# Seven block products instead of eight in the first feed-forward matrix, with fewer filler matmuls at the start

## The reference, cut to what matters

```
h2 = rms_norm(x, norm2[l]) * (1.0 + sc2) + sh2
hidden = jnp.square(jax.nn.relu(h2 @ w_ff1[l]))      # (512 x 1024) @ (1024 x 4096)
x = x + gt2 * (hidden @ w_ff2[l])                    # (512 x 4096) @ (4096 x 1024)
```

## Time and profile before

| | |
|---|---|
| median of 3 runs | 3221.87 us |
| the profiled execution | 3222.51 us |
| its span in the trace | 3220.8 us |
| TensorE matmul busy | 3208.4 us (100%), 15398 matmuls |
| VectorE busy | 1898.4 us (59%) |
| ScalarE busy | 1157.6 us (36%) |
| GpSimd busy | 239.1 us (7%) |
| granted TensorE clock | 0.999 |

### The profile page before, as it was taken

The page is one execution under the profiler, slowest core; times in us unless marked ns, Lnnn a source line. Parts: engine busy times, 40 slices in busy tenths (PEclk is TensorE's granted clock), DMA queues, the critical chain, the costliest instruction groups (busy, mean ns, idle before and its releaser), DMA issues.

```text
span 3220.8 us, 43689 instructions
## 1 busy us (share of the span) xinstructions
PE 3208.4 (100%) x15398; PEld 2653.5 (82%) x15398; DVE 1898.4 (59%) x2738; ACT 1157.6 (36%) x1534; POOL 239.1 (7%) x250
## 2 busy tenths in 40 slices
PE   9999999999999999999999999999999999999998
PEld 8788888888888788888888888768888888888887
DVE  8455557554447455567564445666665744586656
ACT  4433343332223433333332223354333523553423
POOL 2100000100001100000100002051000101320001
PEclk9999999999999999999999999999999999999999
DMA  7246325322222146325422222202222322122222
GB/s 266 67 167 209 120 96 171 136 98 96 93 98 99 63 163 206 129 92 169 141 95 98 98 98 90 79 27 102 101 98 96 107 98 92 47 79 99 97 98 79
DMA packets 100012, 358.89 MB, mean 111 GB/s; under 512 B 11056, under 2 KB 13360, under 8 KB 99760
## 3 DMA queue, kind: packets, MB, share of 16 engines
q1 hardware_dynamic: 98960, 354.08, 31.5%
q0 software_dynamic: 928, 3.17, 0.3%
HBM read 355.11 MB, written 2.10 MB: 111 GB/s over the span
## 4 chain that ended last, share of the span: by engine, by line
PE 99%; DVE 1%; ACT 0%; DVEq 0%; issue 0%; ACTq 0%; POOL 0%; POOLq 0%
PE pb L625 25%; PE pb L626 25%; PE pb L627 25%; PE pb L657 2%; PE pb L658 2%; PE pb L661 2%; PE pb L695 2%; PE pb L696 2%; PE pb L697 2%; PE pb L1014 1%; PE pb L1388 1%; PE pb L1389 1%; PE pb L1390 1%; PE pb L920 1%; PE pb L1004 1%; PE pb L921 1%
## 5 line engine op out<-in xcount | busy, mean ns | idle before, releaser
L1460 ACT ACTIVATE hi<-raw 128x1024 fp32r<-128x1024 f32 x548 | 576.4, 1056 | 983.4 <-PE pb L627 674.1
L2010 DVE TENSOR_TENSOR lo<-raw,hi 128x1024 fp32r<-128x1024 f32 x548 | 668.5, 1224 | 352.6 <-ACT hi L1460 307.8
L625 PE MATMUL pb<-yH,hi 128*128 128x512 f32 (+1 forms) x1664 | 645.1, 388 | 0.0
L626 PE MATMUL pb<-yL,hi 128*128 128x512 f32 (+1 forms) x1664 | 644.8, 388 | 0.0
L627 PE MATMUL pb<-yH,lo 128*128 128x512 f32 (+1 forms) x1664 | 644.8, 388 | 0.0
L625 PE MATMUL pb<-hH,hi 128*128 128x512 f32 x1512 | 590.7, 391 | 0.0
L626 PE MATMUL pb<-hL,hi 128*128 128x512 f32 x1512 | 589.2, 390 | 0.0
L627 PE MATMUL pb<-hH,lo 128*128 128x512 f32 x1512 | 589.1, 390 | 0.0
L626 PEld LDWEIGHTS pb<-yL,hi 128*128 128x128 f32 x1664 | 312.6, 188 | 63.5
L627 PEld LDWEIGHTS pb<-yH,lo 128*128 128x128 f32 x1664 | 312.6, 188 | 63.5
L625 PEld LDWEIGHTS pb<-yH,hi 128*128 128x128 f32 x1664 | 312.7, 188 | 63.3
(11 more groups left out here) (438 smaller groups left out, 4038.8 us busy)
## 6 DMA issues: line engine op xcount, KB each, us to landing
raw<-stream SPq DMA_DIRECT2D x648, 512.0 KB, 3.3
yF<-first SPq DMA_DIRECT2D x8, 512.0 KB, 12.3
act<-first SPq DMA_DIRECT2D x8, 512.0 KB, 15.6
x<-xT SPq DMA_DIRECT2D x4, 512.0 KB, 6.4
outT<-act SPq DMA_DIRECT2D x7, 256.0 KB, 2.2
act<-crow POOLq DMA_DIRECT2D x2, 512.0 KB, 5.6
tab<-decay SPq DMA_DIRECT2D x1, 1024.0 KB, 8.1
scr<-ws POOLq DMA_DIRECT2D x2, 256.0 KB, 3.1
```

The source lines that it names most:

```text
L625: pe.matmul(out, whi, ahi, start=first, stop=False)
L626: pe.matmul(out, whi, alo, start=False, stop=False)
L1460: act.activation(hi[:, s], raw[:, s], ACT.Copy).then_inc(hi_ready, 1)
L2010: dve.tensor_tensor(lo[:, s, 0:width], raw[:, s, 0:width], hi[:, s, 0:width].bitcast(F32), ALU.subtract).then_inc(lo_ready, 1)
```

## The change

**Block products.** In slabs two to four, two weight tiles are worked together as a group. The weights of a group are cut in four quarters (`raw[:, s0]` and `raw[:, s1]` hold the two output blocks, each with its two inner halves), and the input h2 (`hH`, `hL`) is cut in inner half by token half. Seven products of quarters take the place of eight. Each product is 4 inner blocks x 3 matmuls, of 128 x 256. The sums of quarters are made so:

- of h2 once per layer: `token_sums` on GpSimd, ten tensor_tensor of 128 x 1024, then `token_hi` (ScalarE) and `token_lo` (VectorE);
- of the weights for each group: `weight_sums` on GpSimd, four tensor_tensor of 128 x 512, then `fast_hi` part 2 (ScalarE, 128 x 1536) and the last line of `fast_lo` (VectorE, 128 x 1536).

The seven results are put together in PSUM by accumulation, three copies of ScalarE (`keep`), and four adds and a copy of VectorE. The relu, the square and the rounding are done by ScalarE (`hidden_out`), the low part by VectorE (`hidden_rest`). There are 2 layers x 3 slabs x 4 groups = 24 groups.

**Fillers.** `warm_up` has 6 matmuls instead of 16. In `first_norm` the fillers ahead of and between the five sums go, and 6 + 6 stand after them instead of 8 + 4.

```diff
+            def token_sums(l):
+                pool.wait_ge(h_ready, KT - POOL_RESTS + 16 * (2 * l + 1))
+                b = lambda n, k, t: (hH, hL)[n][:, KH[k], TH[t]].bitcast(F32)
+                pool.tensor_tensor(t_raw[1], b(0, 0, 1), b(0, 0, 0), ALU.subtract)
+                pool.tensor_tensor(t_raw[3], b(0, 1, 1), b(0, 0, 1), ALU.subtract)
...
+                pool.tensor_tensor(t_raw[4], t_raw[4], b(1, 1, 0), ALU.add)
+                pool.drain().then_inc(t_sums, 1)
+
+            def weight_sums(l, j, g):
...
+                pool.wait_ge(landed[s0], 16 * (n // RING + 1))
+                pool.wait_ge(landed[s1], 16 * (n // RING + 1))
+                if fast_at(l, j, g) >= 2:
+                    pool.wait_ge(p_full, 5 * (fast_at(l, j, g) - 1))
+                pool.tensor_tensor(e3, a11, a21, ALU.subtract)
+                pool.drain()
+                pool.tensor_tensor(a21, a21, a22, ALU.add)
+                pool.drain().then_inc(s1_ready, 1)
+                pool.tensor_tensor(e2, a21, a11, ALU.subtract)
+                pool.drain()
+                pool.tensor_tensor(e4, a12, e2, ALU.subtract)
+                pool.drain().then_inc(w_sums, 1)
...
                 sum_squares()
+                token_sums(l)
+                pool.wait_ge(t_lo, l + 1)
+                for j in FAST_SLABS:
+                    for g in range(FAST_GROUPS):
+                        weight_sums(l, j, g)
...
             def warm_up():
 
                 pe.wait_ge(fill_ready, 1)
-                for _ in range(16):
+                for _ in range(6):
...
             def first_norm():
 
-                keep_busy(6, 1)
                 for k in (0, 1):
                     pe.wait_ge(squared, k + 1)
                     pe.matmul(pb[:, 4], mean_col.to_broadcast([P, P]), A[:, k], start=k == 0, stop=False)
-                    keep_busy(2, 1)
...
+            def fast_group(l, j, g):
...
+                def product(out, weights, tokens, first=True):
+                    (wH, wL), (aH, aL) = weights, tokens
+                    for k in range(4):
+                        w = slice(k * P, (k + 1) * P)
+                        for n, (wP, aP) in enumerate(((wH, aH), (wH, aL), (wL, aH))):
+                            ins = pe.matmul(out, wP[:, w], aP[:, k], start=first and k == n == 0, stop=k == 3 and n == 2,
+                                            skip_group_check=not first)
+                    return ins
+                pe.wait_ge(lo_ready, tiles.next())
+                pe.wait_ge(bank_free, banks.next(2))
+                product(one_sum, ring_part(s0, 0), quarter(0, 0)).then_inc(p_full, 1)
+                pe.wait_ge(lo_ready, tiles.next())
+                if j == 1 and g == 0:
+                    pe.wait_ge(t_lo, l + 1)
+                product(other_sum, ring_part(s1, 0), (tokH[1], tokL[1])).then_inc(p_full, 1)
...
+                product(pb[:, d0, 0:256], ring_part(s0, 1), quarter(1, 0)).then_inc(tile_done, 1)
+                product(pb[:, d0 + 1, 0:256], ring_part(s1, 1), (tokH[4], tokL[4])).then_inc(tile_done, 1)
+                pe.wait_ge(e_lo, at + 1)
+                pe.wait_ge(p_kept, 3 * at + 1)
+                product(one_sum, extra(2), (tokH[2], tokL[2]), False).then_inc(p_full, 1)
+                pe.wait_ge(p_kept, 3 * at + 2)
+                product(other_sum, extra(4), quarter(1, 1), False).then_inc(p_full, 1)
+                pe.wait_ge(p_kept, 3 * at + 3)
+                product(one_sum, extra(3), (tokH[3], tokL[3]), False).then_inc(p_full, 1)
...
-                with repeat(pe, 3, {tiles: 16, banks: 16, y_k: 8}):
+                for j in FAST_SLABS:
                     tiles_T(8, yH, yL, (y_ready, y_k.value()))
                     y_k.next(8)
-                    tiles_T(8, hH, hL, None)
+                    for g in range(FAST_GROUPS):
+                        fast_group(l, j, g)
...
+            def fast_slab(l, j):      # ScalarE
...
+                for g in range(FAST_GROUPS):
+                    s0, s1 = 2 * (g % 2), 2 * (g % 2) + 1
+                    if g:
+                        hidden_out(g - 1, 0)
+                        hidden_out(g - 1, 1)
+                    keep(g, 0, s0)
+                    if g + 1 < FAST_GROUPS:
+                        fast_hi(l, j, g + 1, 0)
...
+                    keep(g, 1, s1)
+                    if g + 1 < FAST_GROUPS:
+                        fast_hi(l, j, g + 1, 1)
+                        fast_hi(l, j, g + 1, 2)
...
+                    keep(g, 2, s0)
```

More of the change, by code:

```diff
@@ L30 @@
 TILE = KT * P
+FAST_SLABS, FAST_GROUPS = (1, 2, 3), 4
 N_ADA = 6 * D // P
@@ L337, in build @@
         x_added = sem("x_added")
+        t_sums = sem("t_sums")
+        t_hi = sem("t_hi")
+        t_lo = sem("t_lo")
+        s1_ready = sem("s1_ready")
+        w_sums = sem("w_sums")
+        e_hi = sem("e_hi")
+        e_lo = sem("e_lo")
+        p_full = sem("p_full")
+        p_kept = sem("p_kept")
+        d_ready = sem("d_ready")
+        hidden_hi = sem("hidden_hi")
         y_ready = sem("y_ready")
@@ L1572, in to_late, with token_hi, fast_hi @@
                 return work
+            def token_hi(l):
+                act.wait_ge(t_sums, l + 1)
+                for n in (1, 2, 3, 4):
+                    act.activation(tokH[n], t_raw[n], ACT.Copy)
+                act.drain().then_inc(t_hi, 1)
+            def fast_hi(l, j, g, part):
+                at, q = fast_at(l, j, g), g % 2
+                if part == 2:
+                    act.wait_ge(w_sums, at + 1)
+                    act.activation(halved[:, eH_at(q)], act3[:, e_at(q)], ACT.Copy).then_inc(e_hi, 1)
+                    return
+                s = 2 * q + part
+                act.wait_ge(landed[s], land[s].next(16))
+                if part:
+                    act.wait_ge(s1_ready, at + 1)
+                act.wait_ge(tile_done, split.next())
+                act.activation(hi[:, s], raw[:, s], ACT.Copy).then_inc(hi_ready, 1)
@@ L1744, in _ @@
                 tiles_T(8, lambda i, s: to_st(s), peel=True)
-                with repeat(act, 3, {split: 16, done: 16, stf: 8, **{c: 64 for c in land}}):
-                    tiles_T(8, lambda i, s: None, uses_st=False)
-                    tiles_T(8, lambda i, s: to_st(s))
+                token_hi(l)
+                for j in FAST_SLABS:
+                    down_slab(l, j)
+                    fast_slab(l, j)
                 if l < LAYERS - 1:
@@ L2226, in add_to_x, with token_lo, fast_lo @@
                 tiles_T(n, add, last=last, peel=peel, from_bank=True)
+            def token_lo(l):
+                dve.wait_ge(t_hi, l + 1)
+                for n in (1, 2, 3, 4):
+                    ins = dve.tensor_tensor(tokL[n], t_raw[n], tokH[n].bitcast(F32), ALU.subtract)
+                ins.then_inc(t_lo, 1)
+            def fast_lo(l, j, g):
+                at, q = fast_at(l, j, g), g % 2
+                for s in (2 * q, 2 * q + 1):
+                    land[s].next(16)
+                    dve.wait_ge(hi_ready, split.next())
+                    if s == 2 * q:
+                        dve.wait_ge(w_sums, at + 1)
+                    dve.tensor_tensor(lo[:, s], raw[:, s], hi[:, s].bitcast(F32), ALU.subtract).then_inc(lo_ready, 1)
+                dve.wait_ge(e_hi, at + 1)
+                dve.tensor_tensor(halved[:, e_at(q)], act3[:, e_at(q)], halved[:, eH_at(q)].bitcast(F32), ALU.subtract
+                                  ).then_inc(e_lo, 1)
@@ new lines, in down_slab @@
+            def down_slab(l, j):
+                for n in range(KT):
+                    if n < 5:
+                        tick(n % RING)
+                    elif n == 6:
+                        fast_lo(l, j, 0)
+                    drained.next()
+                    dve.wait_ge(tile_done, done.next())
+                    dve.scalar_tensor_tensor(x[:, n], pb[:, n % RING], mod[:, 40 + n:41 + n], x[:, n], ALU.mult, ALU.add
+                                             ).then_inc(bank_free, 1)
@@ L2536, in _ @@
                 tiles_T(8, hidden, peel=True)
-                with repeat(dve, 3, {split: 16, drained: 16, done: 16, **lands(4)}):
-                    add_to_x(8, gate=40)
-                    tiles_T(8, hidden)
+                token_lo(l)
+                for j in FAST_SLABS:
+                    down_slab(l, j)
+                    fast_slab(l, j)
                 if l < LAYERS - 1:
```

104 lines of the change are left out of this document (100 added, 4 removed).

## The result

The changed kernel takes 3230.34 us (median of 10 runs, 3229.67 to 3231.30), the kernel before 3221.88 us beside it (10 runs). The ratio is 1.0026, with a 95% interval of 1.0018 to 1.0035: 8.5 us slower. Predicted were 3232.5 us and a range of 3206 to 3249. The profiled execution took 3230.28 us, its span is 3228.6 us, 7.8 us longer than that of before.

What follows compares the result with a forecast made beforehand. TensorE, busy the whole span with 99% of the chain, bounds the kernel. 3222.5 - 19.5 + 25.6 + 2.4 + 3.6 - 1.5 = 3233.1 us profiled, so 3232.5 us; range 3206 to 3249.

Steps and rivals of the forecast that it cites:

- Groups: Block products in slabs two to four: a group takes 10.06 us instead of 10.88, 24 groups, -19.5 us.
- Rival D: Matmuls of 256 columns are held by their weight loads in a long stretch: 3311 us; chance 2%.
- Token sums: Head of slab one: GpSimd's ten operations hold up VectorE, so TensorE waits 12.8 us per layer, +25.6 us.
- Rival A: Faster: GpSimd's ten operations are really hidden behind slab one and VectorE loses little, 3204.5 us; chance 22%.
- B: No difference: only operations with two different inputs wait, 6.4 us per layer, no clock loss, 3217.3 us; chance 20%.
- The cast: Head of slab one: VectorE's cast waits for GpSimd too, 12.8 us per layer; without it, 11.2.
- The clock: TensorE falls back to 1.2 GHz at slab one's gaps: 1.2 us per layer, +2.4 us, bounds 0 and 2.9 per layer.
- Waits in the groups: TensorE waits 0.3 us in each of 12 groups, before the seventh product of groups one and two: +3.6 us.
- Rival C: Slower still: the groups stall too, up to 23 us instead of 3.6; 3242 us, at the end 3252; chance 12%.
- The start: With fewer fillers VectorE goes on after the first norm at 16.35 instead of 18.31: -1.5 us, bounds -2 and +2.5.
- the two rows: Measured waits before the change: GpSimd's add at 616.40 took 1.94 us, VectorE's `lo` at 615.74 took 1.44 us.
- the rule of turns: VectorE and GpSimd each wait for the whole of the other's instruction, then do their own; 2.29 us per VectorE operation.

Runs made afterwards that it cites:

- the run with 25 fillers: Changed kernel with 25 filler matmuls ahead of the fifth and of the sixth tile of slab one in each layer: 3226.99 us, ratio 1.0015.
- the pair on one chip: Changed kernel with the ten token sums moved to VectorE behind slab one, with the fewer start fillers 3202.24 us, with the old ones 3203.75 us.

## Why the prediction was right

The time came 2.2 us below the forecast, and its mechanism was the one that held. Term by term:

- **Groups**, predicted -19.5: measured -19.2. The slot of 0.12 us held in the long stretch, with weights loaded for each matmul. Rival D is out.
- **Token sums**, predicted +25.6: 25.0, read where the clock stays at 1.00 (the run with 25 fillers). The waits of layer one were to be 6.4 and 6.3. Counted from start to start they were 6.1, and 4.2 after a tile that ran 1.8 us too long at the low clock, 6.0 together. The first of the two low parts was to end at 670.5, which is 668.9 with the start's shift of 1.6. It ended at 668.5. Rival A is out, and B too, as relu and square wait and the cast does as well. GpSimd's own operations took 2.4 to 3.3 us, not 3 to 3.5.
- **The cast**, which no row of before showed: 2.47 instead of 0.43, so it waits. The Trainium skill's rule (SBUF — State Buffer, Who interferes with whom) held. The same section of the Trainium skill lets an operation with at most one input in SBUF, outside the two-port modes, go free, which the 0.74 and 0.75 of the adds to x agree with.
- **The clock**, predicted +2.4, bounds 0 to 5.8: 3.7 by the traces of the run with 25 fillers, 3.4 by its median. The granted clock fell at all four gaps. As foreseen, what is lost behind the first gap of a layer is hidden in the second wait.
- **Waits in the groups**, predicted +3.6, bounds 0 to 23: measured 0. This is the step that failed. The chain is right, but I made it 0.4 us too long: it was to end 8.8 us after the group's start at 752.72, and ended after 8.44, with the product due after 8.64. The next record begins 0.27 after the start of a copy, where I had put 0.35, and relu, square and rounding came to 3.6 instead of 3.7. With so little on either side, tenths of a microsecond decided between a wait in 12 groups and none. Rival C is out, but the run with a longer chain shows how near it was: 0.9 us more on ScalarE cost 8 us.
- **The start**, predicted -1.5: measured -1.6, and 1.5 in the pair on one chip. The first weight matmuls ran at full rate. The last sum of squares was 0.3 us later than before, which ate part of the 1.96.

The sum of what was measured: -19.2 + 25.0 + 3.7 + 0 - 1.6 = +7.9 us, +7.8 before rounding, where the prediction's terms add up to +10.6. So the small miss in the time is also luck: the groups' 3.6 us too much was partly made up by 1.3 too little for the clock.

Two places of its working are weaker than they look. The 0.02 us to which the two rows follow the rule of turns tests nothing, since the 0.1 to 0.15 us taken off each operation come from the same two rows. What tests the rule is the trace after: the first eight operations of VectorE end within 0.8 us of where it put them. And its own range, 3224 to 3250, isn't the sum of its bounds, which is 3222 to 3258.

What stays open is why layer one's stretch grew by 14.9 us and layer two's by 13.8. It isn't a property of the layers: in the run with ScalarE's longer chain, whose slab one is the same, they grew by 13.8 and 15.0. The first wait is 5.9 us in each of these cases; the second is not, and how long the low clock lasted behind each differs too.

## What to carry to other kernels

An engine that is 7% busy is not free to use. Before giving GpSimd work, look for the stretch in which VectorE has no slack, multiply the number of VectorE's operations in it that read SBUF alone by the length of GpSimd's instruction, and compare this with the slack, not with the shares. Work that may stand anywhere within 40 us belongs where the busier engine has slack, even on that engine: ten operations of 1.22 us on VectorE cost nothing where ten of 2.40 us on GpSimd cost 28 us. And when TensorE waits some microseconds, the wait is not the whole price: in the changed kernel up to half of the next 3.6 to 6 us was lost too, and only narrow windows of the granted clock show it.

## What the runs showed of the hardware that was not expected

- Cutting GpSimd's instructions in half halves what each VectorE operation waits (2.0 us to 0.94) but gained only 3 us of 28, as the number of turns doubles.
- Behind a gap of 3.9 us the granted clock was 0.50 over the next 4.3 us and more. It also fell after shorter ones: 1.0 us after TensorE had gone on behind the gap of 2.96, and 0.8 us after it had gone on behind that of 2.35 in the kernel with halves. Behind the 2.71 us in that kernel's layer two it was 0.50 at once. Behind the waits of 1.3 to 1.7 us in that kernel it stayed at 1.00:

```profile
664.80:672.00 7.20, 5.87 (x25) 1.00 0.22 73
```

- TensorE at 1.2 GHz has its 128 x 256 matmuls 0.213 us apart and its 128 x 512 ones 0.43, against 0.120 and 0.227 at 2.4 GHz. The short ones lose 44% of their rate, the long ones 47%.
